# Norms turned by a diagonal of reciprocal roots, router logits on stationary weights, router and experts in one block

## The chip, the cores and the metric

The kernel runs on one core of one Trainium2 chip. The metric is the device time of one execution in microseconds (us), as the median of several runs. All data is float32. A core has TensorE (matrix products), VectorE, ScalarE, GpSimd and SyncE, which issues the DMA transfers here. In the profile they are PE (with PEld for its weight loads), DVE, ACT, POOL and SP; a trailing q (SPq) means the engine's queue of issues.

## The reference, cut to what matters

A decoder trunk with two layers works on 256 tokens of width 1024. Every layer adds a mixer and a mixture of experts to the stream `h`, each behind an RMS norm, and a fifth RMS norm makes the output.

```
def rms_norm(x, g):  return x * rsqrt(mean(x * x) + 1e-6) * g

for layer in (0, 1):
    u = rms_norm(h, norm_mix[layer])
    h = h + (rwkv7_and_sparse_attention(u) if layer == 0 else mamba2(u))
    h = h + hier_moe(rms_norm(h, norm_ffn[layer]), ...)
return rms_norm(h, norm_final)

def hier_moe(t, wg, bg, we, be, w_gate, w_up, w_down):
    pg = softmax(t @ wg + bg)                 # 4 groups, the best one is taken
    le = (t @ we + be)[chosen group]          # 8 experts in it, the best two are taken
    weights = top2(softmax(le)) / their sum * pg[chosen]
    out = sum over the two experts e:  weight_e * (silu(t @ w_gate[e]) * (t @ w_up[e])) @ w_down[e]
```

There are 32 experts in each layer. One expert has three matrices of 1024 x 512, which are 6 MiB, so a layer of experts reads 192 MiB (201.3 MB) from memory.

## The kernel before

The program is a row of blocks; all engines meet at the border of each: `hyb` (mixer of layer 0), `routerffn0`, `expertsffn0`, `overflowffn0`, `closeffn0`, `ssm` (mixer of layer 1), the same four blocks for `ffn1`, and `final`. Tokens lie on partitions in two halves of 128 (`HALVES`), `h` is `[128, 2, 1024]`.

**A norm.** `norm_act` (L204) lets ScalarE take the sum of squares of both halves (L210, 128x1024 each) and then one square root for both (L213). `norm_dve` (L216) takes one reciprocal (L219) and writes `u = h * reciprocal * gain` for each half (L223). `turn_pe` (L226) transposes `u` with 16 TensorE transposes against the identity (L233), four to a PSUM bank, and `turn_act` (L237) copies each bank to `uT` (L242). The last block has no turning: `u` goes out in one transfer of 1 MiB (L2429 and after). The gain row is loaded (a row repeated on all partitions, 512 KiB) as the first transfer of the block that uses it.

**The router block.** SyncE issues the gain row, the router's weights (1024 x 36), its bias row, and then the 18 chunks of 1 MiB of the first three experts (`load_chunk`, L1384). For each half TensorE multiplies with `uT` as the stationary operand and the 36 columns moving (L1514), and VectorE goes through a chain in which each step waits for the one before: bias, best group, penalty for the other groups, best two experts, weights, and a 0/1 table `hit` of chosen experts. The chain is run for half 0 and then for half 1 (L1442 to L1471). TensorE then counts with triangular and all-one matrices how many earlier tokens chose each expert (L1520 to L1524), VectorE forms `rank`, the position of each token in its expert's list, and the number of tiles (L1477 to L1488). ScalarE copies `u` in another order to `ux` (L1497).

**The experts block.** VectorE writes one-hot tables `sel` and `selw` from `rank` (L1632, L1635), then sorts the experts by their count (L1644 to L1648). The fixed experts 0, 1 and 2 come first, the others follow in order of size, in 16 pairs: nine large ones (64 tokens each, L1716 and L1754) and seven small ones (32 tokens, L1731 and L1768). TensorE gathers the tokens of a pair (L1686), projects, turns, projects down and scatters (L1778). Weights lie in a ring of three experts, six chunks each. SyncE refills a chunk only when TensorE has counted it as used:

```
for c in range(CHUNKS):
    if waits:
        sp.wait_ge(ps.s["used"], USES * (b0 + s - RING) + FREED[c])
    load_chunk(sp, ps, e, ph, c)
```

The ring cannot be filled before the mixer's block is over, since the two share the on-chip memory.

Of the kernel before, what the change touches and what calls it, by code (L numbers as in the profile page):

```python
# [8 lines left out]
U32 = mybir.dt.uint32  # L9
I32 = mybir.dt.int32  # L10
ALU = mybir.AluOpType
# [36 lines left out]
CAP, CAP_S = 64, 32  # L48
DC = 2048
# [7 lines left out]
def columns(spec):  # L57

    at, out = 0, {}
    for name, n in spec:  # L60
# [19 lines left out]
                       ("ssm_d", DI // P), ("ssm_norm", DI // P)])  # L80

ROWS, NROWS = columns([("mix0", D), ("ffn0", D), ("mix1", D), ("ffn1", D), ("final", D), ("gn_w", RW),
                       ("gn_b", RW), ("dt_bias", MH), ("a_log", MH), ("rb0", 36), ("rb1", 36)])
# [60 lines left out]
def build(nc, a, known, new):  # L144
# [59 lines left out]
    def norm_act(act, tag, junk, ss, rstd):  # L204

        for t in range(HALVES):
            act.wait_ge(*at("h", tag, t))
            if t:
                act.wait_ge(act_done, AC.n)  # L209
            nc.scalar.activation(junk[:, :], h[:, t, :], ACT.Square, accum_out=ss[:, t:t + 1]).then_inc(  # L210
                act_done, AC.one(("ss", tag, t)))
        act.wait_ge(act_done, AC.n)
# [3 lines left out]
    def norm_dve(dve, tag, rstd, u, gain, gain_sem, gain_n):  # L216

        dve.wait_ge(*at("std", tag))
        nc.vector.reciprocal(rstd[:, :], rstd[:, :]).then_inc(dve_done, DV.one())  # L219
        dve.wait_ge(gain_sem, gain_n)  # L220
        dve.wait_ge(dve_done, DV.n)  # L221
# [4 lines left out]
    def turn_pe(pe, tag, src, tiles, ready):  # L226

        for t in range(HALVES):
            pe.wait_ge(*at(*ready, t))
            for q in range(tiles // 4):  # L230
                b = take(pe, "turn", tag, t, q)
# [1131 lines left out]
    def experts(layer):  # L1363
# [255 lines left out]
        def dve_pass(dve, ps, b0, p0, plan, looped, table, ids, sorts):  # L1619
# [32 lines left out]
            if sorts:  # L1652
                sort()
# [857 lines left out]
```

## Time and profile before

| | |
|---|---|
| runs | 1553.78, 1545.06 and 1550.3 us, median 1550.3 us |
| profiled execution | 1545.25 us, its span 1543.4 us |
| mean granted TensorE clock | 0.950 of full speed |
| blocks in the span | `hyb` 0 to 264, router to close of layer 0 264 to 769, `ssm` 769 to 1030, router to close of layer 1 1030 to 1532, `final` from 1532 |

The span runs from the first to the last instruction; 1.85 us of the execution lie around it. A row of a timeline merges neighbouring instructions of one line, and xN says how many. A float32 matrix product is recorded as two MATMUL entries, a transpose as one.

### The profile page before, as it was taken

The numbers are of one execution on the slowest core, as the hardware profiler recorded it, in microseconds if no ns is written. First come the engines' busy times: TensorE is split into PE (matmuls) and PEld (weight loads), VectorE is DVE, ScalarE is ACT, GpSimd is POOL, SyncE is SP. The second block draws the span as 40 slices with busy tenths as digits, with TensorE's granted clock in tenths as the row PEclk, the third lists the DMA queues.
The fourth block names the chain that finished last, engine by engine and source line by source line (L and its number), as shares of the span: only waits on it lengthen the run. The fifth ranks groups of instructions, "written<-read, shape, count | busy, mean of one in ns | idle before, by whom it ended". The sixth has DMA issues, their size and how long they took to land. (4 is left out here: it accounts for less than half of the span.)

```text
span 1543.4 us, 22104 instructions
## 1 busy us (share of the span) xinstructions
PE 1391.0 (90%) x8910; PEld 780.0 (51%) x8910; DVE 415.3 (27%) x1058; ACT 283.7 (18%) x528; POOL 10.0 (1%) x12
## 2 busy tenths in 40 slices
PE   6999997699999999988689998986999999999884
PEld 3778883443444444433278886543444444443431
DVE  0148744421112111211135735214111211121111
ACT  2232321210110011100132553212010101110001
POOL 0000000000000000000000010000000000000000
PEclk9989979699999999999889998997999999999997
DMA  9311011999999999999463350149999999999993
GB/s 291 130 56 32 27 56 34 422 421 421 421 422 421 418 414 409 421 421 420 192 225 109 133 195 1 55 147 421 420 422 420 422 422 421 416 421 420 421 421 146
DMA packets 85583, 459.52 MB, mean 298 GB/s; under 512 B 10960, under 2 KB 16208, under 8 KB 36208
## 3 DMA queue, kind: packets, MB, share of 16 engines
q1 hardware_dynamic: 85488, 458.18, 73.6%
q8 instruction: 68, 1.11, 0.3%
q14 instruction: 27, 0.22, 0.0%
HBM read 457.11 MB, written 1.05 MB: 297 GB/s over the span
## 5 line engine op out<-in xcount | busy, mean ns | idle before, releaser
L1716 PE MATMUL bank<-rawffn,xgffn 128*64 128x512 f32 x1152 | 254.2, 594 | 0.0
L1662 DVE TENSOR_TENSOR aTffn<-bank,sgffn 128x256 f32<-128x256 f32 (+1 forms) x64 | 23.4, 366 | 620.8 <-ACT sgffn L1611 620.8
L1731 PE MATMUL bank<-rawffn,xgffn 128*32 128x512 f32 x896 | 134.5, 630 | 32.6 <-DMA rawffn<-in_moe_w_up 16.7
L1716 PEld LDWEIGHTS bank<-rawffn,xgffn 128*64 128x64 f32 x1152 | 81.2, 137 | 156.3 <-issue 154.2
L2272 PE MATMUL bank<-uT,wr 128*128 128x256 f32 x640 | 145.1, 386 | 0.0
L1686 PEld LDWEIGHTS bank<-selffn,uxffn 128*128 128x128 f32 x1024 | 122.4, 196 | 36.3 <-issue 24.7
L1754 PE MATMUL bank<-rawffn,aTffn 128*64 128x512 f32 x576 | 131.5, 598 | 10.2 <-DVE aTffn L1662 10.2
L1686 PE MATMUL bank<-selffn,uxffn 128*128 128x128 f32 (+1 forms) x1024 | 130.7, 282 | 10.9 <-DVE selwffn L1635 9.6
L2272 PEld LDWEIGHTS bank<-uT,wr 128*128 128x128 f32 x640 | 122.9, 194 | 18.6 <-issue 1.9
L1608 ACT COPY gusffn<-bank 128x512 f32<-128x512 f32 x64 | 37.5, 585 | 508.4 <-PE bank L1716 315.6
L1778 PE MATMUL bank<-ysffn,selTffn 64*128 64x512 f32 x512 | 127.2, 615 | 1.7 <-DVE ysffn L1673 1.7
L1731 PEld LDWEIGHTS bank<-rawffn,xgffn 128*32 128x32 f32 x896 | 34.5, 115 | 119.1 <-issue 70.7
L1778 PEld LDWEIGHTS bank<-ysffn,selTffn 64*128 64x128 f32 x512 | 44.1, 186 | 84.8 <-issue 81.3
L1673 DVE COPY ysffn<-bank 128x512 f32<-128x512 f32 x64 | 44.2, 690 | 139.3 <-PE bank L1754 95.1
L1754 PEld LDWEIGHTS bank<-rawffn,aTffn 128*64 128x64 f32 x576 | 38.1, 136 | 78.2 <-issue 61.7
L1594 ACT COPY xgffn<-bank 128x512 f32<-128x512 f32 (+1 forms) x64 | 31.5, 492 | 208.5 <-PE bank L1686 208.5
L1768 PE MATMUL bank<-rawffn,aTffn 128*32 128x512 f32 x448 | 53.9, 598 | 4.9 <-DVE aTffn L1662 4.9
L2403 PE MATMUL bank<-wo,xc 128*128 128x512 f32 x128 | 55.3, 592 | 0.0
L1611 ACT ACTIVATE sgffn<-bank 128x256 f32<-128x256 f32 (+1 forms) x64 | 21.5, 337 | 130.5 <-PE bank L1740 65.5
L944 PE MATMUL bank<-uT,wr 128*128 128x256 f32 x192 | 44.9, 394 | 0.0
L944 PEld LDWEIGHTS bank<-uT,wr 128*128 128x128 f32 x192 | 37.8, 199 | 6.4 <-issue 1.0
L2403 PEld LDWEIGHTS bank<-wo,xc 128*128 128x128 f32 x128 | 24.3, 190 | 29.8 <-issue 29.7
(368 smaller groups left out, 1244.6 us busy)
## 6 DMA issues: line engine op xcount, KB each, us to landing
rawffn<-in_moe_w_gate SPq DMA_DIRECT2D x128, 1024.0 KB, 13.6
rawffn<-in_moe_w_up SPq DMA_DIRECT2D x128, 1024.0 KB, 15.7
rawffn<-in_moe_w_down SPq DMA_DIRECT2D x128, 1024.0 KB, 14.7
wr<-in_ssm_w_in SPq DMA_DIRECT2D x10, 2048.0 KB, 8.8
wr<-in_hyb_w_in SPq DMA_DIRECT2D x5, 2048.0 KB, 8.0
wo<-in_ssm_w_out SPq DMA_DIRECT2D x4, 2048.0 KB, 10.3
wr<-in_hyb_w_in SPq DMA_DIRECT2D x1, 1760.0 KB, 11.0
zz<-in_hyb_w_out SPq DMA_DIRECT2D x1, 1536.0 KB, 7.4
```

Source lines behind the costliest of these rows:

```text
L944: i = T.matmul(b[:, c * SEQ:(c + 1) * SEQ], w[:, k, (2 * j + c) * P:(2 * j + c + 1) * P], uT[:, k, :], start=(k == 0), stop=(k == KD - 1))
L1594: nc.scalar.copy(dst[:, :, 4 * half:4 * half + 4, :].rearrange("p x k s -> p k x s"), bank[SIDE_BANK][:, 0:8 * n].rearrange("p (k x s) -> ...
L1608: nc.scalar.copy(gus[:, :, :], bank[GU_BANK][:, :].rearrange("p (q j) -> p j q", j=4)).then_inc(S["gus"], 1)
L1673: V.tensor_copy(ys[:, :], bank[Y_BANK][:, :]).then_inc(S["y"], 1)
L1686: i = T.matmul(bank[SIDE_BANK][:, k * n:(k + 1) * n].rearrange("p (x s) -> p x s", x=2), ux[:, t, 4 * half + k, :], src[:, t, :, :], start ...
L1716: i = T.matmul(bank[GU_BANK][CAP * m:CAP * m + CAP, :], xg[:, odd, k, :], raw[:, slot, (k % 4) * FH:(k % 4 + 1) * FH], start=(k == 0), sto ...
L1731: i = T.matmul(bank[GU_BANK][CAP_S * c:CAP_S * c + CAP_S, :], xg_s[:, odd, 4 * half + k, :], raw[:, CHUNKS * ph + c, k * FH:(k + 1) * FH], ...
L1754: i = T.matmul(bank[Y_BANK][CAP * n:CAP * n + CAP, :], aT[:, j, :], raw[:, slot, jj * D + n * BANK:jj * D + (n + 1) * BANK], start=(j == 0 ...
L1768: i = T.matmul(bank[Y_BANK][CAP_S * c:CAP_S * c + CAP_S, :], aT_s[:, 2 * half + jj, :], raw[:, slot, jj * D + n * BANK:jj * D + (n + 1) * ...
L1778: i = T.matmul(bank[ACC[2 * t + n]][:, :], selT[CAP * n:CAP * n + CAP, x, t * P:(t + 1) * P], ys[CAP * n:CAP * n + CAP, :], start=start, s ...
L2272: i = T.matmul(b[:, c * SEQ:(c + 1) * SEQ], wr2[:, n % 3, k, (2 * j + c) * P:(2 * j + c + 1) * P], uT2[:, k, :], start=(k == 0), stop=(k = ...
L2403: i = T.matmul(js[t][c][:, :], xc[:, 4 * g + k, t * P:(t + 1) * P], wo2[:, g % 2, k, c * BANK:(c + 1) * BANK], start=(g == 0 and k == 0), ...
```

## The change

Five things are changed, in one edit.

1. **Norms.** Each half gets its own square root, right behind its sum of squares. VectorE multiplies `h` with the gain first (`hg`), before the root is known, then takes the reciprocal of the half and writes a diagonal matrix `diag` with the reciprocals in it. TensorE turns `hg` by a real matrix product with `diag` as the moving operand, where it transposed before; this also applies the reciprocal. The last block multiplies `hg` by the reciprocal on VectorE and sends each half in its own transfer of 512 KiB. ScalarE runs one more small instruction with the root's function ahead of the first sum of squares, and one with the exponential behind the second root of a router's norm (`warm_table`).
2. **Loads.** One `gain` tile serves all five norms and is loaded one norm ahead; the identity is loaded in a transfer of its own; the router's weights (now 64 columns wide, 256 KiB) are loaded in the mixer's block. The first transfers of an expert stage are its 18 chunks, and the next gain row stands behind them.
3. **Logits.** The router's weights are the stationary operand, the tokens of both halves move (256 columns); even and odd k go to two halves of the array's columns and are added when the result is turned back.
4. **One chain for both halves** on VectorE, with fewer steps; the weights, the tile count and the sort come behind the first `sel` tables; `select` and the new `weigh` have an event each.
5. **One block** for router and experts.

```diff
-        nc.scalar.activation(rstd[:, :], ss[:, :], ACT.Sqrt, scale=1.0 / D, bias=eps_n[:, 0:1]).then_inc(
-            act_done, AC.one(("std", tag)))
+            act.wait_ge(act_done, AC.n)
+            nc.scalar.activation(std[:, t:t + 1], ss[:, t:t + 1], ACT.Sqrt, scale=1.0 / D, bias=eps_n[:, 0:1]).then_inc(
+                act_done, AC.one(("std", tag, t)))
...
         for t in range(HALVES):
-            nc.vector.scalar_tensor_tensor(out=u[:, t, :], in0=h[:, t, :], scalar=rstd[:, t:t + 1], in1=gain[:, :],
-                                           op0=ALU.mult, op1=ALU.mult).then_inc(dve_done, DV.one(("u", tag, t)))
+            nc.vector.tensor_tensor(hg[:, t, :], h[:, t, :], gain[:, :], ALU.mult).then_inc(
+                dve_done, DV.one(("hg", tag, t)))
+            dve.wait_ge(*at("std", tag, t))
+            nc.vector.reciprocal(rstd[:, t:t + 1], std[:, t:t + 1]).then_inc(dve_done, DV.one())
+            dve.wait_ge(dve_done, DV.n)
+            if turns:
+                nc.vector.tensor_scalar(diag[:, t, :], C("ident"), rstd[:, t:t + 1], None, ALU.mult).then_inc(
+                    dve_done, DV.one(("u", tag, t)))
...
-                    i = nc.tensor.transpose(b[:, k * P:(k + 1) * P], src[:, t, (4 * q + k) * P:(4 * q + k + 1) * P],
-                                            C("ident"))
+                    i = nc.tensor.matmul(b[:, k * P:(k + 1) * P], hg[:, t, (4 * q + k) * P:(4 * q + k + 1) * P],
+                                         diag[:, t, :], start=True, stop=True)
...
+        def router_sync(sp):
+            for e in range(FIXED):
+                for c in range(CHUNKS):
+                    load_chunk(sp, main_pass, e, e, c)
+            load_gain(sp, NORMS[2 * layer + 2])
...
+            for k in range(KD):
+                lo = LW * (k % 2)
+                i = T.matmul(b[lo:lo + LW, 0:SEQ], rw[:, k, :], uT_[:, k, :], start=(k < 2), stop=(k >= KD - 2))
...
             select(ids, False)
             if sorts:
+                weights_dve(dve)
+                weigh(ids, False)
+                tiles_dve(dve)
                 sort()
...
+                for t in range(HALVES):
+                    sp.wait_ge(*at("u", "final", t))
+                    load(sp, "out", a["out"][0, t * P:(t + 1) * P, :], o_f[:, t, :])
```

## Rows read from the trace of the kernel before

**Rows 1.** The page: the span, and what the DMA engines moved in 40 slices.

```profile
span 1543.4 us, 22104 instructions
...
GB/s 291 130 56 32 27 56 34 422 421 421 421 422 421 418 414 409 421 421 420 192 225 109 133 195 1 55 147 421 420 422 420 422 422 421 416 421 420 421 421 146
```

**Rows 2.** Windows: stretch, length, busy (x) per engine, PEclk, DMA share, GB/s.

```profile
265.00:270.00 5.00, 0.70 (x4) 0.71 (x5) 2.21 (x3) 1.97 (x5) 0.00 (x0) 0.81 0.89 254
...
740.00:752.00 12.00, 9.12 (x46) 2.07 (x40) 0.69 (x1) 0.42 (x1) 0.00 (x0) 0.86 0.81 335
...
1031.00:1038.00 7.00, 2.25 (x11) 2.25 (x12) 2.65 (x3) 3.05 (x7) 0.00 (x0) 0.62 0.90 275
```

**Rows 3.** Timeline, both expert stages: start, us, engine, line, operation [idle before].

```profile
264.36 0.33 SPq L256 DMA_DIRECT2D gainffn<-in_rows  x1
...
265.83 0.43 SPq L1384 DMA_DIRECT2D rawffn<-in_moe_w_gate  x1
...
295.52 3.62 PE L1686 MATMUL bank<-selffn,uxffn 128*128 128x128 f32 x16 [4.77 <-DVE selwffn L1635]
...
299.81 2.05 PE L1686 MATMUL bank<-selffn,uxffn 128*128 128x128 f32 x16 [0.67 <-ACT xgffn L1594]
...
301.80 7.09 PE L1716 MATMUL bank<-rawffn,xgffn 128*64 128x512 f32 x32
...
579.23 3.64 PE L1731 MATMUL bank<-rawffn,xgffn 128*32 128x512 f32 x32 [0.51 <-issue]
...
600.90 3.64 PE L1731 MATMUL bank<-rawffn,xgffn 128*32 128x512 f32 x32 [0.51 <-issue]
...
1030.61 0.34 SPq L256 DMA_DIRECT2D gainffn<-in_rows  x1
```

**Rows 4.** Waits of TensorE from 580 to 750 us: total, times, longest.

```profile
PE bank L1731 <- DMA rawffn<-in_moe_w_up: 8.6, 6, 1.9
```

**Rows 5.** Timeline of the first norm.

```profile
5.71 0.19 ACT L728 COPY front<-h 128x1 f32<-128x1 f32 x1 [3.34 <-DMA h<-in_x]
...
11.67 3.65 PE L233 MATMUL bank<-cst,front 128*128 128x128 f32 x16 [11.67 <-DVE front L223]
...
16.37 11.82 PE L935 MATMUL bank<-wr,uT 128*128 128x512 f32 x27 [1.05 <-ACT uT L242]
```

**Rows 6.** Timeline of the second mixer's norm.

```profile
769.27 1.06 ACT L210 ACTIVATE front<-h 128x1024 f32<-128x1024 f32 x1 [14.46 <-PEq L1887]
...
775.95 3.68 PE L233 MATMUL bank<-cst,front 128*128 128x128 f32 x16 [7.77 <-DMA mpar<-in_rows]
...
780.30 4.12 PE L2326 MATMUL bank<-wdt,uT 128*128 128x32 f32 x32 [0.67 <-ACT uT L242]
```

**Rows 7.** Windows for the clock: during one gather, and right behind those transposes.

```profile
290.00:298.00 8.00, 3.23 (x15) 3.10 (x15) 5.87 (x35) 0.00 (x0) 0.00 (x0) 0.50 1.01 419
...
780.00:781.00 1.00, 0.70 (x7) 0.70 (x7) 0.00 (x0) 0.25 (x1) 0.00 (x0) 0.94 1.03 375
```

**Rows 8.** Groups of instructions in the last block: busy us, mean ns.

```profile
L210 ACT ACTIVATE junk_f<-h 128x1024 f32<-128x1024 f32 x2 | 2.1, 1056 | 13.8 <-PEq L1887 13.7
...
L213 ACT ACT_TABLE_LOAD x1 | 1.3, 1283 | 0.0
...
L213 ACT ACTIVATE rstd_f<-ss_f,eps_n 128x2 f32<-128x2 f32 x1 | 0.3, 295 | 0.0
```

**Rows 9.** Timeline of the last block, its first and last issue.

```profile
1532.11 1.06 ACT L210 ACTIVATE junk_f<-h 128x1024 f32<-128x1024 f32 x1 [13.75 <-PEq L1887]
...
1538.94 0.40 SPq L256 DMA_DIRECT2D out<-o_f  x1
```

**Rows 10.** DMA issues: us from issue to landing.

```profile
out<-o_f SPq DMA_DIRECT2D x1, 1024.0 KB, 4.0
...
gain_f<-in_rows SPq DMA_DIRECT2D x1, 512.0 KB, 3.6
```

**Rows 11.** One line's instructions: duration ns, min, median, max.

```profile
L1997 DVE TENSOR_SCALAR xc<-xr,feat x24: 342/347/355, 793.4 to 885.7; 128x256 f32<-128x256 f32 x24
```

More of the change, by code:

```diff
@@ L256, in load, with load_gain, load_router @@
         eng.dma_start(dst, src).then_inc(s_ld[name], 16)
+    def load_gain(sp, tag):
+        n = NORMS.index(tag)
+        if n:
+            sp.wait_ge(*at("hg", NORMS[n - 1], 1))
+        load(sp, "gain", gain[:, :], row_src(tag))
+    def load_router(sp, layer):
+        load(sp, "rw", rw[:, :, :], a["router"][layer].rearrange("(k p) n -> p k n", p=P))
     hyb = ExitStack()
@@ L1526, in experts, with router_act @@
-        rt_.close()
+        ids = C("slots")[:, 0:EXPERTS]
+        def router_sync(sp):
[3 more added lines that the diff above has]
+            load_gain(sp, NORMS[2 * layer + 2])
+        def router_act(act):
+            S = nc.scalar
+            norm_act(act, tag, junk_, ss_, std_)
+            warm_table(act, ACT.Exp)
+            turn_act(act, tag, uT_, KD)
+            act.wait_ge(*at("logits", tag))
+            S.activation(lgT[:, :], bank_of("logits", tag)[:, 0:SEQ], ACT.Identity, bias=FT(f"rb{layer}")).then_inc(
+                act_done, AC.one(("read", "logits", tag)))
+            act.wait_ge(*at("de", tag))
+            for t in range(HALVES):
+                S.activation(gex[:, t, :], bank_of("folded", tag)[:, t * LG:t * LG + EG], ACT.Exp, bias=ngm[:, t:t + 1],
+                             accum_out=gsum[:, t:t + 1]).then_inc(act_done, AC.one())
+            S.activation(de[:, :], de[:, :], ACT.Exp).then_inc(act_done, AC.one(("rexp", tag)))
+            warm_table(act, ACT.Silu)
@@ new lines, in router_pe @@
+        def router_pe(pe):
+            T = nc.tensor
+            turn_pe(pe, tag, hg_, KD, pool=ACC)
+            pe.wait_ge(s_ld["rw"], 16 * (layer + 1))
+            pe.wait_ge(*at("read", "turn", tag, 1, 1))
+            b = take(pe, "logits", tag, pool=ACC)
+            for k in range(KD):
+                lo = LW * (k % 2)
+                i = T.matmul(b[lo:lo + LW, 0:SEQ], rw[:, k, :], uT_[:, k, :], start=(k < 2), stop=(k >= KD - 2))
+            i.then_inc(pe_done, PE.one(("logits", tag)))
+            pe.wait_ge(*at("read", "logits", tag))
+            b = take(pe, "folded", tag, pool=ACC)
+            for t in range(HALVES):
+                i = T.matmul(b[:, t * LG:(t + 1) * LG], lgT[:, t * P:(t + 1) * P], C("ident64")[:, 0:LG], start=True,
+                             stop=True)
+            i.then_inc(pe_done, PE.one(("folded", tag)))
+            pe.wait_ge(*at("hit", tag))
+            b = take(pe, "rank", tag, pool=ACC)
+            T.matmul(b[:, 0:HALVES * EXPERTS], C("before"), hit[:, :, :], start=True, stop=False)
+            T.matmul(b[:, EXPERTS:2 * EXPERTS], C("ones"), hit[:, 0, :], start=False, stop=True).then_inc(
+                pe_done, PE.one(("rank", tag)))
+            b = take(pe, "count", tag, pool=ACC)
+            for t in range(HALVES):
+                i = T.matmul(b[:, 0:EXPERTS], C("ones"), hit[:, t, :], start=(t == 0), stop=(t == HALVES - 1))
+            i.then_inc(pe_done, PE.one(("count", tag)))
@@ L1637, in select @@
                                             ALU.is_equal, ALU.mult)
-                i.then_inc(S["sel"], 1)
+                i.then_inc(S["selw"], 1)
             def sort():
@@ L1945, in _ @@
         def _(sp):
-            load(sp, "gain", gain2, row_src("mix1"))
             load(sp, "small", wdt[:, :, :], w_ssm[:, :, DI + XBC:DI + XBC + MH])
```

323 lines of the change are left out of this document (159 added, 164 removed).

## The prediction

> **What bounds the kernel now.** I read the page's two bandwidth lines first, then windows at both ends of the expert stages, then the timeline over the start of each stage. The page [rows 1] shows two long plateaus near 421 GB/s, one for each layer's experts, and much lower rates elsewhere. So the kernel has two regimes. In the expert stages the DMA engines stream without a pause; in the mixers, the norms and the last block some chain of engines decides.
>
> The plateau needs care, since TensorE is busy nearly all of that time too. The nine large pairs run from 301.80 to 579.23 us [rows 3], 30.8 us each. A pair reads 12 chunks of 1.049 MB, which at 421.5 GB/s takes 29.9 us. TensorE is thus a little slower than the stream while pairs are large, and much faster when they are small: 600.90 - 579.23 = 21.7 us. It catches up, and from then on it waits for weights [rows 4]. The stage ends when the last chunk lands and one expert's work behind it is done. The time at which a router ends matters only in so far as it stops the stream.
>
> How much does it stop it? Ring slots come free as TensorE uses them. Expert e frees its first chunk about 3.6 us after its start, at 301.8 + 15.4 e + 3.6 us; the stream wants that slot for expert e + 3, at S + 14.9 (e + 3), where S is the stream's start (about 268.6, below). With 2 us from issue to data (my estimate, half of the 4.0 us in which 1 MiB lands [rows 10]) the slot is late from e = 11 or so, and by 18 experts this adds up to some 3 us. The page agrees: after a level of 421.5 the slices from 501 to 617 us have 418, 414 and 409 [rows 1], which is 38.6 x (3.5 + 7.5 + 12.5) / 421.5 = 2.2 us of lost stream. In layer 1 one slice has 416, so 0.5 us.
>
> **The start of a stage.** In layer 0 the first issue is at 264.36, but that is the gain row; the first chunk is issued at 265.83 [rows 3], behind the gain, the router's weights and its bias row. From 265 to 270 us the engines moved 254 x 5 = 1.27 MB [rows 2], of which 0.69 MB is those three small loads. The 0.58 MB of chunks would take 1.4 us at full rate, so the stream starts in effect at 268.6, 4.3 us behind the first issue. In layer 1 it is 275 x 7 - 690 = 1235 KB by 1038 [rows 2], in effect a start at 1035.1, 4.5 us behind the first issue at 1030.61 [rows 3]. The other end checks this: 335 x 12 = 4.02 MB after 740 us puts the end of layer 0's stream at 749.5. From 268.6 that is 480.9 us, against 201.3 MB / 421.5 = 477.6 us plus the 2.2 us found above.
>
> **What the change does there.** The chunks become the first issues. What does a first transfer need before the engines run? From 265 to 270 their busy share is 0.89 [rows 2], so they stood empty for at most 0.55 us of it and were at work from 265.5, 1.2 us behind the gain's issue. I take 1.3 us, and as bounds 1.0 and the 2.4 us by which a load of 512 KiB (1.2 us at full rate) lands later than its size explains [rows 10]. That saves 4.3 - 1.3 = 3.0 us in layer 0 and 3.2 us in layer 1. Behind the 18 chunks stands a new gain row, 0.52 MB, so 1.2 us come back in each. The faster router takes away the late slots. Before, the first gather is at 295.52, 31.2 us behind the block's start, and the first projection at 37.4. I count after: small root, sum of squares and root 1.9 us, reciprocal and diagonal 0.5; 16 real products at 16 recorded MATMULs in 3.62 us for eight [rows 3], so 7.2 us; last eviction 0.7; eight products with 256 columns, in two column halves at a time, 3.4; bias copy, turning back and evictions 1.5; some 16 small VectorE steps at 0.2 to 0.3 make 3.8 (the old chain needed two such rounds in a row); ranks 1.2, copy and `sel` 1.3. The sum is near 22 us, so the first projection comes 9 us earlier, and the slot is late only from e = 11 + 9 / 0.46, beyond the 18 large experts. The lost 2.2 and 0.5 us vanish (bounds: half of it stays, or all goes). Experts: -(3.0 - 1.2 + 2.2) = -4.0 and -(3.2 - 1.2 + 0.5) = -2.5 us. The ScalarE copies to `ux` go to VectorE, ahead of the logits, and hide behind TensorE's turning; without that cover they would cost the 4 us or less by which the router is still far from the limit. A third scalar operand in `select` and the split into `sel` and `selw` lie under 20 us of TensorE per pair: nothing.
>
> **The norm at the start.** Before: x is there at 5.71, turning starts at 11.67, the first group at 16.37, 1.05 us behind the last transpose [rows 5]. After: table load 1.28, small root 0.3, square 1.2, root 0.3 [rows 8], reciprocal and diagonal 0.5, so half 0 is ready at 9.6, two us earlier. But 16 products are 32 recorded MATMULs where 16 were. A gather of the same shape shows both prices: 3.62 us for 16 records at a granted clock of 0.50, 2.05 us at full [rows 3, 7]. The 16 transposes took 3.65 us, the price per record of the lower one. Turning then takes 7.2 us if all of it is at 1.2 GHz, and 5.7 if the second half is at 2.4. The first group starts at 17.9 or 16.4, against 16.37. The first weight group leaves little to gain: 5.1 MB stand in the queue up to its end, 12.1 us even at the plateau's rate, behind a start of some 2 us. I take +0.5 (bounds -0.5 and +1.5).
>
> **The norm of layer 1's mixer.** Before, the block starts at 769.27, turning starts at 775.95, held by the small loads and not by `u`, and the next products start at 780.30, 0.67 us behind the last transpose [rows 6]. After, turning no longer waits for those loads. Half 0 is ready 3.7 us into the block; 32 records end at 10.9 with the lower clock throughout or at 9.4 with the upper in the second half; the next products start at 11.6 or 10.1, where it was 11.0. Right behind the old transposes the clock was granted at 0.94 [rows 7], so the upper level is within reach. I take -0.3 (bounds -1.5 and +1.0).
>
> **The last block.** It starts at 1532.11 and issues its output at 1538.94, 6.8 us in [rows 9]. After: 1.28 + 0.3 + 1.2 + 0.3 = 3.1 for the first root, 4.6 for the second. VectorE: reciprocal and scaling of half 0 to 4.2, product of half 1 (1.3) to 5.5, reciprocal 0.2, scaling 0.8, issue at 6.5. The scaling of 1024 columns isn't in the trace: 0.35 us for 256 [rows 11] bounds it below, four times that (1.4) above, and I take 0.8, since a fixed part must be in the 0.35. The last transfer is then 512 KiB, and such a one landed in 3.6 us where 1 MiB took 4.0 [rows 10]. Sum: -0.3 - 0.4 = -0.7 (bounds -1.6 and +0.9).
>
> Two rules of the Trainium skill bear on this block. "VectorE: DVE Perf Modes", section "The perf-mode tier table (the rule you actually need)", has float32 `tensor_scalar` between on-chip tiles at twice the rate of a product of two tensors, 1227 ns for 2048 columns; half of that would be an estimate of 0.6 us for the scaling, and by it the block would gain 1.1 us and not 0.7. "DMA: Bandwidth & Descriptors", section "Bandwidth", speaks against the change: it asks for transfers of 1 MiB or more, and the output is now cut into two of half that size. By it the second half would gain nothing on the whole, and the block would gain 0.3 us. No row here shows a written half.
>
> **Sum.** -4.0 - 2.5 + 0.5 - 0.3 - 0.7 = -7.0 us against the profiled execution's 1545.25 us (span 1543.4 and 1.85 around it), so 1538.3. That execution stands at the fast edge of the runs shown, whose median is 1550.3; the same difference from the median gives 1543.3 us, 0.45% less. About 0.5%, 7.8 us, is what a measurement of this kernel can tell from no change. The runs before spread over 8.7 us.
>
> Other moved steps: the router's weights and the gain row are now issued in the mixers, ahead of the attention's compression weights and, in layer 1, ahead of the fourth weight group. They add 0.8 MB, under 3 us of queue. TensorE works without a gap over weights that landed before (from 16.37 on [rows 5]), so I put nothing; without that cover it would be up to 3 us.
>
> **Rivals.**
> - *No measurable change* (forecast, 0.50): the stream is what bounds, and only its start moves. Own range 1540 to 1549.
> - *The small terms all fall well* (0.27): the clock rises within the turning, scaling is cheap, the first block wins a us. -4.5 - 3 + 0 - 1.5 - 1.6 = -10.6, so 1540.
> - *The router counts in full* (0.13): if the stream is late because TensorE is and never catches up, both stages end 9 and 7 us earlier, -16 - 0.5 = -17, so 1533. For it: SyncE's issues wait for TensorE through the large pairs. Against it: the waits for weights in the small ones [rows 4].
> - *Slower by the clock* (0.10): TensorE catches up earlier and waits more in the small pairs, the granted clock falls to 1.2 GHz, and a small pair takes up to 43 us where the stream needs 29.9. Each such pair at the end of a stage costs 13 us, so from one and a half of them on the gain is gone; with two, -7 + 26 = +19, so 1569. Against it: TensorE already waits there, and the plateau holds [rows 1, 4].
>
> Chances: faster by over 0.5% 0.40, within 0.5% 0.50, slower 0.10. The range runs from the full router, 1533, to a gain of nothing with one spread of the runs, 1552.
>
> **What would show it.** The first chunk issued at the block's start, and the stream at full rate 1.3 us later; no slice below 420 in the plateaus; the plateaus as long as before less 3 us; the first projection 28 us into the block; turning in 5.7 to 7.2 us; the last issue at 6.5 us of the last block. It is wrong if the expert stages shrink by 8 us or more, or if the small pairs run with a clock near 0.5.

## The result and the profile after

| | before | after |
|---|---|---|
| median of 17 runs each | 1551.8 us | 1541.8 us |
| lowest to highest | 1545.1 to 1555.2 | 1537.7 to 1550.6 |
| profiled execution, its span | 1545.25, 1543.4 us | 1538.1, 1536.3 us |
| mean granted TensorE clock | 0.950 | 0.961 |

The ratio is 0.9938, with a 95% interval of 0.9924 to 0.9952: 0.6% faster, 10 us. The 1543.3 us of the prediction is 1.5 us off and the range holds the result. Part of that is luck: the median of before rose from 1550.3 to 1551.8 us with more runs. The gain is 10 us where 7 were forecast, and "no change beyond 0.5%" was the wrong side of a narrow line.

The page of the changed kernel, against [rows 1], and its count of the transfers that the profile calls instruction (packets, MB, share), used further down:

```profile
span 1536.3 us, 22145 instructions
...
GB/s 288 155 55 19 40 57 26 423 420 422 420 422 421 421 422 420 421 421 420 190 240 118 145 176 1 65 166 420 421 421 421 422 422 421 421 420 422 421 420 120
...
q8 instruction: 67, 1.10, 0.3%
```

No slice within the plateaus is under 420 now; the 418, 414, 409 and 416 of before are gone. Windows of the changed kernel at both ends of the expert stages and over the second mixer's start (columns as in [rows 2]):

```profile
265.00:270.00 5.00, 3.04 (x27) 3.04 (x28) 4.65 (x8) 4.91 (x11) 0.00 (x0) 1.00 0.82 297
...
736.00:752.00 16.00, 12.24 (x82) 4.74 (x84) 1.87 (x4) 1.14 (x3) 0.00 (x0) 1.00 0.67 278
...
773.00:777.00 4.00, 3.23 (x26) 3.07 (x25) 0.00 (x0) 1.66 (x3) 0.00 (x0) 0.91 1.05 393
777.00:781.00 4.00, 4.00 (x31) 3.85 (x31) 0.81 (x4) 0.56 (x1) 0.00 (x0) 1.00 1.04 386
781.00:785.00 4.00, 4.00 (x21) 3.51 (x20) 0.00 (x0) 2.63 (x5) 0.00 (x0) 1.00 1.05 389
...
1025.00:1030.00 5.00, 3.45 (x17) 3.45 (x18) 4.65 (x8) 4.24 (x9) 0.00 (x0) 0.66 0.92 331
...
1495.00:1511.00 16.00, 12.31 (x65) 3.62 (x65) 1.58 (x3) 0.86 (x2) 0.00 (x0) 0.89 0.71 295
```

The same arithmetic as in the prediction: 297 x 5 = 1.49 MB take 3.5 us at the plateau's rate, so the stream of layer 0 starts in effect at 266.5; 278 x 16 = 4.45 MB put its end at 746.6, 481.7 us behind the block's start at 264.81. Before, it was 749.5 - 264.36 = 485.2. In layer 1 it starts in effect at 1026.1 and ends at 1506.2, 481.8 us in.

The timeline of the changed kernel, from the first norm to the last block, to be held against [rows 3, 5, 6, 9]:

```profile
7.83 1.23 DVE L235 TENSOR_TENSOR front<-h,gain 128x1024 f32<-128x1024 f32 x1 [6.82 <-DMA gain<-in_rows]
...
9.51 5.29 PE L254 MATMUL bank<-diag,front 128*128 128x128 f32 x32 [9.51 <-DVE diag L241]
...
16.66 3.67 PE L972 MATMUL bank<-wr,uT 128*128 128x512 f32 x8 [1.87 <-DMA wr<-in_hyb_w_in]
...
264.81 0.33 SPq L1422 DMA_DIRECT2D rawffn<-in_moe_w_gate  x1
...
266.96 3.84 PE L254 MATMUL bank<-diag,hgffn 128*128 128x128 f32 x32 [3.24 <-DVE diag L241]
...
271.52 1.95 PE L1477 MATMUL bank<-uTffn,rw 128*64 128x256 f32 x16 [0.72 <-issue]
...
279.52 3.75 PE L1747 MATMUL bank<-selffn,uxffn 128*128 128x128 f32 x16 [0.98 <-DVE hitsffn L1554]
...
287.67 7.76 PE L1778 MATMUL bank<-rawffn,xgffn 128*64 128x512 f32 x32
...
744.67 3.62 PE L1793 MATMUL bank<-rawffn,xgffn 128*32 128x512 f32 x26 [2.12 <-DMA rawffn<-in_moe_w_up]
...
769.08 6.05 PE L254 MATMUL bank<-diag,front 128*128 128x128 f32 x32 [5.02 <-DVE diag L241]
775.90 3.73 PE L2396 MATMUL bank<-wdt,uT 128*128 128x32 f32 x32 [0.77 <-ACT uT L263]
779.47 14.06 PE L2342 MATMUL bank<-uT,wr 128*128 128x256 f32 x64
...
1504.66 5.08 PE L1793 MATMUL bank<-rawffn,xgffn 128*32 128x512 f32 x26 [1.43 <-DMA rawffn<-in_moe_w_up]
...
1530.38 0.75 DVE L244 TENSOR_SCALAR o_f<-o_f,rstd_f 128x1024 f32<-128x1024 f32 x1
...
1531.16 2.33 SPq L277 DMA_DIRECT2D out<-o_f  x2
```

The first projection (L1778) starts 22.9 us into the block, where it was 37.4. The last projection of each layer is worth a look: the same 26 records take 3.62 us in layer 0 and 5.08 in layer 1. The landing of the output, from the list of issues of the changed kernel:

```profile
out<-o_f SPq DMA_DIRECT2D x2, 512.0 KB, 2.7
```

### The profile page after: what moved, and what is told of

The parts are those of the page before. It is cut to its first block and busy times, and to the rows that moved or that the text cites. A ratio compares the mean times of both kernels' runs of the same rounds, so it can differ in the third digit from the quotient of the medians.

```text
span 1536.3 us, 22145 instructions
## 1 busy us (share of the span) xinstructions
PE 1403.4 (91%) x8946; PEld 780.2 (51%) x8946; DVE 418.7 (27%) x1025; ACT 278.1 (18%) x538; POOL 10.0 (1%) x12
## 5 line engine op out<-in xcount | busy, mean ns | idle before, releaser
L1778 PE MATMUL bank<-rawffn,xgffn 128*64 128x512 f32 x1152 | 255.6, 596 | 0.0
L1793 PE MATMUL bank<-rawffn,xgffn 128*32 128x512 f32 x896 | 147.5, 647 | 42.3 <-DMA rawffn<-in_moe_w_up 22.2
L1778 PEld LDWEIGHTS bank<-rawffn,xgffn 128*64 128x64 f32 x1152 | 81.4, 138 | 157.6 <-issue 155.7
L1747 PEld LDWEIGHTS bank<-selffn,uxffn 128*128 128x128 f32 x1024 | 125.8, 200 | 28.7 <-issue 26.8
L1747 PE MATMUL bank<-selffn,uxffn 128*128 128x128 f32 (+1 forms) x1024 | 134.3, 287 | 3.3 <-DVE hitsffn L1554 2.0
L2342 PEld LDWEIGHTS bank<-uT,wr 128*128 128x128 f32 x640 | 121.7, 192 | 18.1 <-issue 1.9
## 6 DMA issues: line engine op xcount, KB each, us to landing
rawffn<-in_moe_w_gate SPq DMA_DIRECT2D x128, 1024.0 KB, 24.4
```

Of the source, the lines that this page charges most:

```text
L1747: i = T.matmul(bank[SIDE_BANK][:, k * n:(k + 1) * n].rearrange("p (x s) -> p x s", x=2), ux[:, t, 4 * half + k, :], src[:, t, :, :], start ...
L1778: i = T.matmul(bank[GU_BANK][CAP * m:CAP * m + CAP, :], xg[:, odd, k, :], raw[:, slot, (k % 4) * FH:(k % 4 + 1) * FH], start=(k == 0), sto ...
L1793: i = T.matmul(bank[GU_BANK][CAP_S * c:CAP_S * c + CAP_S, :], xg_s[:, odd, 4 * half + k, :], raw[:, CHUNKS * ph + c, k * FH:(k + 1) * FH], ...
L2342: i = T.matmul(b[:, c * SEQ:(c + 1) * SEQ], wr2[:, n % 3, k, (2 * j + c) * P:(2 * j + c + 1) * P], uT2[:, k, :], start=(k == 0), stop=(k = ...
```

## The experiments

Twelve runs were made: eight edits of the changed kernel, the changed kernel once more, and the kernel before three times more. Each was profiled once, and a single profile can be several us off in a block that is not edited. So this table of block lengths, worked out from the first instruction of each block in each trace, is needed for every reading below. "Stream end" is worked out as above, in us behind the block's start; "last" is the duration of the last projection (26 records), first of layer 0, then of layer 1.

| kernel | mixer 0 | experts 0 | mixer 1 | experts 1 | last block | stream end | last |
|---|---|---|---|---|---|---|---|
| before | 264.4 | 504.9 | 261.4 | 501.5 | 11.4 | 485.2, 483.7 | 5.0, 3.6 |
| before, 2nd | 269.9 | 505.2 | 261.7 | 501.7 | 11.4 | 485.3, 483.6 | 5.1, 3.6 |
| before, 3rd | 262.6 | 503.5 | 261.8 | 501.6 | 11.4 | 484.1, 483.6 | 3.6, 3.6 |
| before, 4th | 263.8 | 504.9 | 261.8 | 502.1 | 11.4 | 485.1, 483.6 | 5.1, 3.6 |
| after | 264.8 | 500.8 | 258.7 | 502.9 | 9.0 | 481.7, 481.8 | 3.6, 5.1 |
| after, 2nd | 269.5 | 503.5 | 262.5 | 503.2 | 9.0 | 481.7, 481.8 | 5.9, 5.1 |
| loads back | 266.1 | 504.0 | 264.7 | 503.6 | 11.1 | 483.2, 483.6 | 5.3, 3.6 |
| router 14 us late | 269.5 | 507.3 | 258.9 | 506.1 | 9.0 | 487.8, 486.7 | 3.6, 5.2 |
| router 29 us late | 267.9 | 521.0 | 258.8 | 520.1 | 9.0 | 500.5, 499.8 | 5.3, 5.1 |
| transposes | 266.5 | 500.1 | 261.9 | 500.6 | 9.0 | 481.8, 481.7 | 3.6, 3.6 |
| filled waits | 268.5 | 501.2 | 258.7 | 500.8 | 9.0 | 481.5, 481.8 | 3.6, 3.6 |
| output whole | 265.6 | 502.8 | 262.4 | 503.2 | 10.4 | 481.7, 481.7 | 5.3, 5.3 |
| busy turn | 268.1 | 503.4 | 260.1 | 501.6 | 9.0 | 481.7, 481.9 | 6.1, 3.6 |
| busy and filled | 270.2 | 501.5 | 260.8 | 503.0 | 9.0 | 481.6, 481.9 | 3.6, 3.6 |

The last block repeats within 0.1 us, and the stream end within 0.4 where its edit leaves the stream alone, but for 1.2 us in layer 0 of before. The first mixer's block scatters over 7 us before the change and over 5 with it.

**Theories.** A, the prediction's: in the expert stages the stream bounds, so the kernel gains by the earlier start and by the late slots that vanish, and little from a faster router. Rival B: the router counts in full. For the rest: the clock, or the work itself.

**Loads back where they were.** Gain rows and router weights are loaded again at the start of the block that uses them; all else is as changed.

```diff
-            load_router(sp, 0)
-            load_gain(sp, "ffn0")
...
         def router_sync(sp):
+            load_gain(sp, tag)
+            load_router(sp, layer)
             for e in range(FIXED):
                 for c in range(CHUNKS):
                     load_chunk(sp, main_pass, e, e, c)
-            load_gain(sp, NORMS[2 * layer + 2])
```

> The changed kernel with the moved loads put back: gain row and router weights are issued in the block that uses them, ahead of the 18 chunks, and the gain of layer 1's mixer and of the last block at the start of their blocks. Stream theory (an expert stage is as long as its stream of weights): the stream starts 4.3 us into the block instead of 1.65 and carries 1.2 us less behind it, so each expert stage is 1.4 to 1.9 us longer than in the changed kernel; the two norms that now wait for a gain row landing 3.6 us into the block are each about 2 us later; in all +7 us. Rival (the ring hides a late start of the stream, since three experts are loaded ahead): the expert stages stay as they are and only the two norms cost, +4 us.

Measured: 1553.5 us (10 runs), ratio to before 0.9986, interval 0.9958 to 1.0014. Windows of this kernel at both ends of layer 0's stage, and then its timeline in the second mixer:

```profile
266.00:271.00 5.00, 0.00 (x0) 0.00 (x0) 0.47 (x1) 4.35 (x9) 0.00 (x0) 0.87 0.79 201
737.00:753.00 16.00, 12.17 (x64) 3.77 (x64) 1.58 (x3) 0.53 (x2) 0.00 (x0) 0.89 0.78 323
```

```profile
775.59 6.71 PE L254 MATMUL bank<-diag,front 128*128 128x128 f32 x32 [7.18 <-DVE diag L241]
```

The stream's end goes back by 1.5 and 1.9 us, the last block by 2.1, since VectorE's product waits for the gain row, and in the second mixer turning starts 5.6 us into the block where it was 3.4. The ratio rises by 0.48%, 7.4 us of the 9.6 that the ratio of the change stands for; +7 was expected. By the two intervals the 7.4 is known to some 5 us either way, so the firmer evidence is that the times of these places moved as expected. Moving the loads is most of the change. The other four parts together leave a ratio that can't be told from 1, which leaves room for up to 6.5 us. The kernel before with the loads alone moved was not run.

**The router made late.** VectorE does 12 or 24 products of 1024 columns whose result nobody reads, ahead of the first `sel`; the faster router is thus given back, and more.

```diff
+            for _ in range(12):
+                did(V.tensor_tensor(junk_[:, :], h[:, 0, :], h[:, 1, :], ALU.mult))
```

> The changed kernel with 12 products of 128x1024 (1.22 us each, 14.6 us, results not used) on VectorE between ranks and the first sel tables of each router, so that the first projection starts as late as in the kernel before. Stream theory: only slots freed late count. With the stream's start S and the first projection P, the lost stream is P - S - 39.2 + 0.46 x 18 us, when positive: 4.9 us in layer 0 and 6.5 in layer 1, +11 us in all at the most; if it is as in the kernel before, +2.5. Rival (the router's time counts in full): +29 us.

> As the run before, with 24 products, 29 us per router. Stream theory: P - S is now near 50, so the slots are late from the first expert on; loss 19.5 and 21 us by the same formula, +40 us in all, and the weight stream shows a hole after its first 18 chunks. Rival in full: +58 us.

Measured: with 12 products 1552.0 us, ratio 0.9975 (0.9949 to 1.0001), first projection 40.0 and 39.5 us into the blocks. With 24 (one run) 1578.7 us. The page and a window of the kernel with 24 products, and its timeline:

```profile
span 1576.8 us, 22193 instructions
...
GB/s 287 146 54 39 18 55 68 422 302 413 410 414 402 411 409 409 421 421 421 210 238 109 149 170 1 94 173 333 397 412 413 400 413 411 410 409 421 420 421 137
```

```profile
755.00:777.00 22.00, 17.45 (x98) 5.72 (x94) 1.90 (x5) 1.14 (x3) 0.00 (x0) 0.92 0.62 258
```

```profile
283.57 30.20 DVE L1546 TENSOR_TENSOR junkffn<-h 128x1024 f32<-128x1024 f32 x24
...
314.93 3.75 PE L1749 MATMUL bank<-selffn,uxffn 128*128 128x128 f32 x16 [30.81 <-DVE hitsffn L1556]
```

With 15.1 us of delay (half of the 30.20) the streams end 6 and 5 us later, with 30.2 us 18.7 and 18.1. The first projection stands at 53.4 and 52.7 us with 24 products. From 12 to 24 products it thus moves by 13.4 and 13.2 us, and the stream's end follows by 12.7 and 13.1, nearly in full. Taking the loss from the place of the first projection gives the same point four times: 40.0 - 6.0, 39.5 - 5.0, 53.4 - 18.7 and 52.7 - 18.1 are 34.0 to 34.7 us into the block. That is a threshold, as in A: a late router costs only from the point at which TensorE frees a chunk after the stream wants it, and then for each of the nine large pairs (plateaus of 400 to 414). B would have cost 15.1 us for each half. The changed kernel, whose first projection starts 22 to 24 us into the block in its two profiles, stands some 10 us before that point. The expectation's formula gives 7.4 and 6.9 us for the places measured with 12 products, and 20.8 and 20.1 for 24: right in kind, 1.4 to 2.1 us too high.

**Turning by transposes.** VectorE multiplies `hg` by the reciprocal and TensorE transposes it against the identity, as before. The edit also has the waits that this needs, and copies `ux` without the factor.

```diff
-                nc.vector.tensor_scalar(diag[:, t, :], C("ident"), rstd[:, t:t + 1], None, ALU.mult).then_inc(
+                nc.vector.tensor_scalar(hg[:, t, :], hg[:, t, :], rstd[:, t:t + 1], None, ALU.mult).then_inc(
...
-                    i = nc.tensor.matmul(b[:, k * P:(k + 1) * P], hg[:, t, (4 * q + k) * P:(4 * q + k + 1) * P],
-                                         diag[:, t, :], start=True, stop=True)
+                    i = nc.tensor.transpose(b[:, k * P:(k + 1) * P], hg[:, t, (4 * q + k) * P:(4 * q + k + 1) * P],
+                                            C("ident"))
```

> The changed kernel, but hg is multiplied by the reciprocal on VectorE (0.75 us per half instead of 0.29 for the diagonal) and turned by transposes against the identity, 16 recorded MATMULs per norm instead of 32. Theory of records (the product with the diagonal costs twice the TensorE time): layer 1's mixer starts its groups about 1.5 us earlier, the first norm gains nothing since its first group waits for weights, the routers are off the path: -1.5 us. Rival (the longer product work is what has the clock at full for the first group of layer 1's mixer): that group takes 15.4 us again instead of 14.1, net 0 to +1.5 us.

Measured: 1541.8 us, ratio 0.9924 (0.9901 to 0.9946). Its timeline in the first norm and the second mixer:

```profile
10.02 3.88 PE L254 MATMUL bank<-cst,front 128*128 128x128 f32 x16 [10.02 <-DVE front L241]
16.66 3.64 PE L972 MATMUL bank<-wr,uT 128*128 128x512 f32 x5 [2.76 <-DMA wr<-in_hyb_w_in]
...
770.55 3.97 PE L254 MATMUL bank<-cst,front 128*128 128x128 f32 x16 [5.49 <-DVE front L241]
775.28 7.01 PE L2397 MATMUL bank<-wdt,uT 128*128 128x32 f32 x32 [0.77 <-ACT uT L263]
782.10 15.81 PE L2343 MATMUL bank<-uT,wr 128*128 128x256 f32 x64
```

In the whole the diagonal gives nothing that can be measured. The first norm's next products start at 16.66 with either, held by their weights. In the second mixer transposing is 2.1 us shorter, but `dt` then takes 7.01 us where the changed kernel had 3.73, the group behind it takes 15.81 and not 14.06, and the block is 261.9. That is the rival of the expectation: the shorter work is given back by the clock.

**Filled waits.** In the last four small pairs of a stage TensorE does a product of 512 columns that nobody reads, before each wait for the third and the fourth chunk of an expert.

```diff
+                            if fill and k == 0 and c >= 2:
+                                if odd:
+                                    pe.wait_ge(S["pt"], p0 + t + 1)
+                                T.matmul(bank[SIDE_BANK][:, :], C("ones"), cst[:, 0:BANK], start=True, stop=True)
```

> The changed kernel with one more float32 product of 512 columns on TensorE (0.88 us at full clock, result not used) ahead of the waits for the third and the fourth chunk of each expert in the last four small pairs of both layers, where TensorE waits for weights 1.2 to 2.1 us. Clock theory (part of the time behind the last chunk, and of the scatter between runs, is TensorE at the lower clock after such waits: the last projection took 5.08 us in layer 1 and 3.62 in layer 0): -1 to -3 us against the changed kernel, and a smaller scatter. Rival (the clock there does not matter, only the landing of the last chunk does): 0, or up to +1 us if the added products are not hidden.

Measured: 1540.1 us (6 runs), ratio 0.9927 (0.991 to 0.9945), mean granted clock 0.965 to 0.971 over the six. Timeline of both last projections:

```profile
746.64 1.05 PE L1797 MATMUL bank<-rawffn,xgffn 128*32 128x512 f32 x2
747.61 1.13 PE L1794 MATMUL bank<-cst 128*128 128x512 f32 x2
748.93 3.62 PE L1797 MATMUL bank<-rawffn,xgffn 128*32 128x512 f32 x26 [0.20 <-DMA rawffn<-in_moe_w_up]
...
1508.35 3.62 PE L1797 MATMUL bank<-rawffn,xgffn 128*32 128x512 f32 x26 [0.38 <-DMA rawffn<-in_moe_w_up]
```

Both at the upper level, as in the later run with filled waits: four of four. Without the filling six of the sixteen in kernels with the changed norms were at 3.6 us. Four of four alone could be chance. But all 28 stage ends (two in each of the 14 profiles) can be sorted by how long TensorE waits for weights ahead of the last projection, over the last two or three waits: of the seven with 2.1 us or less in all (four of them filled) none is slow, of the twelve with 2.8 to 2.9 us five are, of the nine with 3.2 to 3.9 us eight are. So the clock at the end of a stage does follow TensorE's waits, though not strictly, and the low level costs 1.5 us or more in the projection. But the gain in the median can't be told from nothing.

**Output in one transfer.**

```diff
-                for t in range(HALVES):
-                    sp.wait_ge(*at("u", "final", t))
-                    load(sp, "out", a["out"][0, t * P:(t + 1) * P, :], o_f[:, t, :])
+                sp.wait_ge(*at("u", "final", 1))
+                load(sp, "out", a["out"][0].rearrange("(t p) d -> p t d", p=P), o_f[:, :, :])
```

> The changed kernel with the output in one transfer of 1 MiB behind the second half, as before. Theory (the last transfer's size sets its landing: 2.7 us for 512 KiB here, 4.0 for 1 MiB before): +1.3 us in the last block, whose length goes from 9.0 to 10.3 us. Rival (halves below 1 MiB are less efficient, and the landing is mostly a fixed time): +0.4 us or less.

Measured: 1543.0 us (4 runs), ratio 0.9947 (0.9926 to 0.9967). Its timeline and its list of issues:

```profile
1539.82 0.41 SPq L277 DMA_DIRECT2D out<-o_f  x1
```

```profile
out<-o_f SPq DMA_DIRECT2D x1, 1024.0 KB, 4.0
```

The issue comes 5.9 us into the block and the landing takes 4.0 us, as before the change. The block is 10.4 us, against 9.0 with halves: the halves are worth 1.4 us there. The medians can't resolve that.

**TensorE kept busy ahead of the turning.** Three products of 512 columns at the start of the second mixer's block, in the 3.4 us in which TensorE waits for the first diagonal; then the same with the filled waits; and beside them the changed kernel again.

```diff
-            pe.wait_ge(*at("u", tag, t))
+            if t:
+                pe.wait_ge(*at("u", tag, t))
...
+                if t == 0 and q == 0:
+                    for _ in range(busy):
+                        nc.tensor.matmul(b[:, :], C("ones"), cst[:, 0:BANK], start=True, stop=True)
+                    pe.wait_ge(*at("u", tag, 0))
```

> The changed kernel with three more float32 products of 512 columns (all ones times a constant) on TensorE at the start of the second mixer's block, ahead of the norm's products; they write a bank that the first turning product overwrites, and fill the 3.4 us in which TensorE waits for the first diagonal. Theory A (the mixer's block got shorter because TensorE's clock comes up earlier): the granted clock comes up before or early in the turning, the 32 turning records take about 4 to 5 us instead of 6.05, the `dt` products 3.73 and the first group of `wr` products 14.1, and the block takes 256.5 to 258 us against 258.75. Theory B (the block is set by its weights' transfers or by VectorE, and the clock only goes along with it): the turning gets faster or not, and the block stays at 258.7 within 0.3 us or goes back to 261 or more, as the extra products end later than the diagonal is ready (they take 2.7 us at the lower level, of 3.4). Expert stages as with the change, 500 to 503 us each.

> The three extra products of the run above, and the filling products in the last four small pairs of each expert stage as in the run with filled waits. If both causes are what they seem, the effects add: expert stages near 500.8 us each with the last projection at 3.6 us in both layers, the second mixer's block at or below 258.7, so 1.5 to 3 us less than the changed kernel in the median, ratio to the kernel before 0.992 or below. If the clock in these places is chance and not TensorE's waits, the ratio is 0.993 to 0.994, that of the changed kernel.

> The changed kernel itself, unedited, beside the two runs above on the same chip: ratio to the kernel before 0.992 to 0.995. If the short block of the second mixer (258.75 us) was chance of that one profile, this profile has 261 to 262 us there and a first projection group of over 15 us; if it is the change's own, it is within 0.3 us of 258.75 again. The last projections of the two expert stages may each be 3.6 or 5.1 us.

Measured, six runs each: 1543.4 us, ratio 0.9923 (0.9896 to 0.995); 1542.6 us, 0.9919 (0.9895 to 0.9942); the changed kernel 1544.0 us, 0.9924 (0.9898 to 0.995). Timeline and a window of the first of them, and of the changed kernel's second profile:

```profile
776.83 3.88 PE L259 MATMUL bank<-diag,front 128*128 128x128 f32 x32
781.48 4.76 PE L2401 MATMUL bank<-wdt,uT 128*128 128x32 f32 x32 [0.77 <-ACT uT L268]
786.05 16.39 PE L2347 MATMUL bank<-uT,wr 128*128 128x256 f32 x64
```

```profile
784.00:788.00 4.00, 4.00 (x16) 3.64 (x16) 0.61 (x3) 0.96 (x1) 0.00 (x0) 0.50 1.04 386
```

```profile
776.40 6.32 PE L254 MATMUL bank<-diag,front 128*128 128x128 f32 x32 [5.02 <-DVE diag L241]
...
783.49 5.58 PE L2396 MATMUL bank<-wdt,uT 128*128 128x32 f32 x32 [0.77 <-ACT uT L263]
788.88 15.53 PE L2342 MATMUL bank<-uT,wr 128*128 128x256 f32 x64
```

```profile
784.00:788.00 4.00, 4.00 (x25) 4.00 (x25) 0.19 (x1) 0.00 (x0) 0.00 (x0) 0.63 1.04 387
788.00:792.00 4.00, 4.00 (x14) 3.44 (x14) 0.61 (x3) 2.10 (x4) 0.00 (x0) 0.52 1.04 387
```

My expectation was half wrong. The turning did get fast, 3.88 us against 6.05. But the three products took 5.5 us and not 2.7 (three times 0.88 is the price at the upper level, and they ran at the lower), so turning started 5.3 us into the block, and behind it the clock fell to 0.50 from 784 on, in `dt` and the first group. The block was 260.1 and 260.8 us. The effects did not add: with both edits layer 1's expert stage was 503.0 us although its last projection took 3.62, since 19.0 us went by behind that projection where all other 27 stage ends have 17.0 to 18.1; why is not known. Nor can the three ratios be told from each other. The changed kernel itself had 262.5 this time: its 258.7 was one of two outcomes of the same code. It goes with whether the granted clock, once up in the turning, drops again for some 5 us (0.63 and 0.52 here from 784 to 792) or stays at 1.00, as in the first profile from 777 on. TensorE waits 0.77 us between turning and `dt` in both. What differs ahead of it is how soon the clock rose: where the turning took 6.04 to 6.14 us the level held (four profiles), where it took 6.32 or 6.61 it dropped (two).

**The kernel before, three more profiles.** These tell how far its first profile can be taken for it.

> The kernel before, unedited, profiled once more. Its first profile had block lengths 264.4, 504.9, 261.4, 501.5 and 11.3 us (mixer 0, experts 0, mixer 1, experts 1, last block). Theory A (turning by transposes leaves the second mixer's block at the longer of its lengths): 261 to 262.5 us here too. Theory B (the block has both lengths whatever turns the norm): about 259 in some of the profiles. The first block, whose code the change touches only in its norm, scattered from 264.8 to 270.2 us in profiles with the change; if the change makes it longer, it stays at 264.4 within a us here, and if the clock does, it scatters as widely: 264 to 270. Last block 11.3 within 0.3 us. Where the last projection of a layer runs at the lower clock, about 5 us against 3.6, that layer's stage is about 2 us longer.

> The kernel before once more, as the run above: three profiles of it then stand against eight of kernels with the change's first block. Expected by A: second mixer 261 to 262.5 us; by B: one of the two is near 259. First block: 264 to 270 if the clock sets it, 264 to 265 if the change lengthened it.

> The kernel before a fourth time. Its timed executions have a median of 1552 to 1554 us at a mean granted clock of 0.948, while its three profiles took 1545.3, 1551.6 and 1542.6 us at 0.950, 0.951 and 0.955. If what a usual execution has more lies in the first mixer's block, that block is 268 us or longer here and the others repeat (505, 261.6, 501.6, 11.3); if it lies in the expert stages, their last projections are the slow ones (over 5 us in both layers) and the stages are 505 and 503.5.

Measured: 1551.6, 1542.6 and 1545.8 us. The second profile's last projections and the next rows of its second mixer:

```profile
751.97 5.06 PE L1731 MATMUL bank<-rawffn,xgffn 128*32 128x512 f32 x26 [1.44 <-DMA rawffn<-in_moe_w_up]
...
782.34 3.55 PE L233 MATMUL bank<-cst,front 128*128 128x128 f32 x16 [8.34 <-DMA mpar<-in_rows]
786.57 4.80 PE L2326 MATMUL bank<-wdt,uT 128*128 128x32 f32 x32 [0.68 <-ACT uT L242]
791.18 16.37 PE L2272 MATMUL bank<-uT,wr 128*128 128x256 f32 x64
...
1517.62 3.62 PE L1731 MATMUL bank<-rawffn,xgffn 128*32 128x512 f32 x26 [1.45 <-DMA rawffn<-in_moe_w_up]
```

With transposes the second mixer is 261.4 to 261.9 us in all five profiles (four of before, one with transposes). With the diagonal and the loads early it is 258.7 to 258.9 in four and 262.4 or 262.5 in two, 260.0 in the mean. The first mixer's block, 262.6 to 269.9, scatters as widely before as after (264.8 to 270.2), so none of it can be laid to the change. What a usual execution has more was not found: the fourth profile's first block was 263.8, its expert stages 504.9 and 502.1. The second profile, the only one as long as the median, has its extra 5.5 us in the first mixer.

## Why the prediction came out as it did

By its own steps; where a mean is given, it is over the profiles named:

- **The stream bounds: right.** Its end moved by -3.4 and -1.9 us (485.17 to 481.73 and 483.71 to 481.80); predicted -4.0 and -2.5. The start saved 2.6 and 2.8 us (266.5 is 1.7 behind the first issue, 1026.1 also), predicted 3.0 and 3.2: the first transfer needs 1.7 us and not 1.3. The gain row took its 1.2 us back and the late slots vanished: -2.6 + 1.2 - 2.2 = -3.6, and -2.8 + 1.2 - 0.5 = -2.1, each within 0.2 of the measured end.
- **From there to the end of the stage: a step I left out.** I let the stage end one expert's work behind the last chunk. The last projection moved less than the stream's end. It starts 2.2 to 3.2 us ahead of that end in the four profiles of before, and 1.3 to 2.6 in five after (the two of the change, transposes, output whole, busy turn), since it waits for an up chunk that now lands later relative to the last. So of -3.4 and -1.9 us, about -2.1 and -0.6 reach it. Then it runs at one of two clocks. In layer 1 it had the upper one in all four profiles of before, and in two of the five after. The stages of these five are 502.1 and 502.3 us in the mean, against 504.6 and 501.7: -2.5 and +0.6. Layer 1 gained nothing in the profiles. The traces show what goes with the later landing of the up chunk. Over the last 49 chunks of all 28 stages the landings follow each other in 2.3 to 2.9 us, 2.49 in the mean, but for 37 intervals of over 2.9 and up to 4.2 us. In each of these 37, or up to 1.5 us ahead of it, a transfer of the kind instruction starts, though the stretches have only 176 of these for 1344 intervals. The last one of a stage starts 3.1 to 3.7 us behind the landing of the last up chunk in all eight stages of before, so it can delay only chunks that the projection does not wait for. In both profiles of the changed kernel it starts 2.9 to 11.6 us ahead of that landing. This is read from the traces, and no run moved such a transfer.
- **The first projection at 28 us: it came at 22.9 and 24.4.** In layer 0 the turning was at the upper clock (3.84 us, not 7.2; 5.36 in layer 1), and the logits took 1.95 us and not 3.4. It changed nothing, as the late router showed.
- **The first norm, +0.5 (bounds -0.5 to +1.5): right.** 16.66 against 16.37, +0.3, and held by `wr` and not by turning.
- **The second mixer, -0.3 (bounds -1.5 to +1.0): the size was off.** Against 261.7, the mean of four, it is -2.9 or +0.8, by the clock, and -1.7 in the mean of six. The step "right behind the old transposes the clock was at 0.94, so the upper level is within reach" priced the level for the turning alone. What counts is the 18 to 21 us of products behind it: the first group takes 14.06 us where the level holds and 15.4 to 16.7 where it drops.
- **The last block, -0.7 (bounds -1.6 to +0.9): mis-sized, -2.4 measured.** The issue came 5.9 us in, where it was 6.8, and not 6.5, and the half landed in 2.7 us, not 3.6. The 3.6 was taken from a gain row that came with the block, a read repeated over the partitions; it was no price for a write. The scaling took 0.75, as the 0.8 assumed. Half of the 1227 ns that the Trainium skill, "VectorE: DVE Perf Modes", section "The perf-mode tier table (the rule you actually need)", gives for 2048 columns had made an estimate of 0.6 us; the measurement decides. The Trainium skill, "DMA: Bandwidth & Descriptors", section "Bandwidth", asks for 1 MiB or more, by which the halves would have had no gain; the run with one transfer shows them to be worth 1.4 us. Here nothing else is in the queue, and it is the last piece's landing that counts, 2.7 us against 4.0.
- **The sum.** -2.5 + 0.6 + 0.3 - 1.7 - 2.4 = -5.7 us by these means, -7.0 predicted. That these are close is luck: the expert stages gave 1.9 us and not 6.5, and the second mixer and the last block 3.1 more than predicted. The medians say -10.
- **The rivals.** "The router in full" is refuted. "Slower by the clock" happens, in one projection and not in whole pairs: 1.5 to 2.5 us and not 13. "The small terms all fall well" is nearest to what was measured, though not by its terms: only the last block and one outcome of the second mixer went that way.

**What stays open** are some 4 us between the blocks' sum and the medians. The four profiled executions of the kernel before are 1545.3, 1551.6, 1542.6 and 1545.8 us, 1546.3 in the mean. The two other executions of it beside the last three profiles, each on the chip of its neighbours, took 1556.7 and 1554.4, and its medians are 1549.6 to 1554.4. The changed kernel's two profiles, 1538.1 and 1549.5 us, lie on both sides of its medians, 1541.8 and 1544.0. The mean clock goes with it: 0.950, 0.951, 0.955 and 0.951 in the profiles of before, 0.942 to 0.954 in its other executions, 0.957 to 0.963 in the changed kernel's six beside the busy turn. So the profiles of before show a kernel 3 to 8 us faster than its medians, and the part of the gain that lies there has no place in any trace that I have. The profiles alone would give a gain of 2.5 us (1544.5 against 1542.0 in mean span). The size of the gain rests on the timed runs: 17 against 17 give 7 to 12 us by their interval, and six more of the changed kernel give a ratio of 0.9924 (0.9898 to 0.995). The loads put back, which cost 7.4 us between two changed kernels, speak for the larger number too. If the other blocks have their mean lengths, the first mixer takes 270.6 us in the median execution before the change and 266.5 after it; no trace shows whether that is so.

None of the versions beats the changed kernel by an amount that its interval resolves.

## What to carry to other kernels

Where a stream of transfers bounds a stage, look at what its queue issues first: 0.7 MB of small loads in front of the first chunk made the stream start 2.6 to 2.8 us later in each stage, and they could be loaded a block earlier. Look also at what the stage's end waits for: it was the last up chunk, and it gained 2.1 and 0.6 us where the stream's end gained 3.4 and 1.9. A faster step beside the stream is worth something only up to the point at which its lateness stops the stream; compute that point from the ring's slots, and expect nothing beyond it. Profile the kernel before more than once: one profile put an unchanged block 5 us away from the next, which is more than half of a gain of 0.5%.

## What the runs showed of the hardware that was not expected

- The same 26 records take 3.62 us or 5.0 to 6.1, in neighbouring executions of one kernel. The longer TensorE waits for weights ahead of them, the more often they are slow: none of seven with waits of 2.1 us or less in all, five of twelve with 2.8 to 2.9, eight of nine with 3.2 to 3.9.
- After a rise to the upper level the granted clock can drop to 0.50 again for 4 to 7 us though TensorE had waited only 0.7 to 0.8 us ahead of it and is busy throughout the drop (4.00 of 4.00 us from 784 to 788 and from 788 to 792 in the second profile of the change). In four profiles it did not drop behind the same wait.
- Chunks of 1 MiB landed every 2.49 us. All 37 intervals of 2.9 to 4.2 us among 1344 had a transfer of the kind instruction starting in them or up to 1.5 us ahead; most of these transfers (136 of 176) showed no such delay.
- A product of 512 columns with both operands constant took 1.8 us at the lower clock (5.46 us for the three), so three of them did not fit into the gap of 3.4 us.
- An output of 512 KiB landed in 2.7 us, one of 1 MiB in 4.0, with nothing else in the queue; the last block was 1.4 us shorter for it (9.0 against 10.4).
